# TensorE's order and the order of the weight loads in the emptier experts of a mixture of experts

## The reference

```python
logits = (t @ router)
top_logits, top_idx = lax.top_k(logits, 2)
gates = softmax(top_logits)
for e in range(8):
    out += combine[:, e:e+1] * (silu(t @ w_gate[e]) * (t @ w_up[e])) @ w_down[e]
```

## Time and profile before

| what | value |
|---|---|
| median of three runs | 3641.31 us (3640.61 to 3642.34) |
| the profiled execution's own time | 3644.42 us |
| its span | 3642.5 us |
| mixture of experts, first product to end of the span | 2402 to 3642.5 us |
| TensorE busy, share of the span | 3203.3 us, 88% |
| weights moved by SP's queue | 612.49 MB, most of them in the last third |

### The profile page before, as it was taken

The page is one execution under the profiler, slowest core; times in us unless marked ns, Lnnn a source line. Parts: engine busy times, 40 slices in busy tenths (PEclk is TensorE's granted clock), DMA queues, the critical chain, the costliest instruction groups (busy, mean ns, idle before and its releaser), DMA issues.

```text
span 3642.5 us, 40190 instructions
## 1 busy us (share of the span) xinstructions
PE 3203.3 (88%) x16779; PEld 2258.2 (62%) x16779; DVE 902.0 (25%) x1854; ACT 487.0 (13%) x1111; POOL 106.9 (3%) x115
## 2 busy tenths in 40 slices
PE   7999987999999997996888998989679859958965
PEld 3565666577777774775755777678348537726832
DVE  1677777300101332003651002210000000000000
ACT  1322231100100231002111002210000000000000
POOL 0121121000000000000000000000000000000000
PEclk8999998999999998998989999989889979979987
DMA  6444411344445222442103452179789779889975
GB/s 208 145 161 174 161 54 47 116 148 150 149 151 167 81 70 93 150 138 94 44 12 117 160 184 70 47 266 316 269 287 320 257 256 347 271 270 314 304 244 174
DMA packets 474993, 636.26 MB, mean 175 GB/s; under 512 B 11094, under 2 KB 419261, under 8 KB 467525
## 3 DMA queue, kind: packets, MB, share of 16 engines
q1 hardware_dynamic: 469645, 612.49, 50.4%
q0 software_dynamic: 5184, 21.46, 1.8%
HBM read 632.70 MB, written 1.20 MB: 174 GB/s over the span
## 4 chain that ended last, share of the span: by engine, by line
PE 78%; DMA 7%; DVE 6%; issue 2%; DVEq 2%; ACT 2%; PEld 1%; PEldq 1%; SPq 1%; ACTq 0%; POOL 0%
PE PS L718 28%; PE PS L726 14%; PE PS L3377 7%; PE PS L1071 4%; DMA scratch<-in_moe_wu 3%; PE PS L3409 3%; DMA WO<-in_moe_wu 2%; PE PS L2941 2%; PE PS L541 2%; PE PS L1625 1%; PE PS L1621 1%; DMA WO<-in_ada_w 1%; PE PS L1879 1%; PE PS L1200 1%; PE PS L280 1%
## 5 line engine op out<-in xcount | busy, mean ns | idle before, releaser
L745 DVE TENSOR_TENSOR scratch<-scratch,PS 128x128 f32<-128x128 f32 (+1 forms) x200 | 69.3, 346 | 1410.3 <-ACT scratch L735 1409.9
L718 PE MATMUL PS<-XT,WF 128*128 128x256 f32 x1472 | 324.6, 381 | 1.4 <-ACT XT L486 1.4
L718 PEld LDWEIGHTS PS<-XT,WF 128*128 128x128 f32 x1472 | 281.0, 191 | 51.4 <-issue 12.0
L718 PE MATMUL PS<-XT,WO 128*128 128x256 f32 x1344 | 296.0, 379 | 0.0
L718 PEld LDWEIGHTS PS<-XT,WO 128*128 128x128 f32 x1344 | 255.3, 190 | 49.3 <-issue 16.3
L735 ACT ACTIVATE scratch<-PS 128x128 f32<-128x128 f32 (+1 forms) x200 | 64.8, 324 | 1391.7 <-PE PS L718 1391.7
L3377 PE MATMUL PS<-XT,scratch 128*64 128x256 f32 x512 | 137.5, 431 | 127.8 <-DMA scratch<-in_moe_wu 127.8
L1071 PE MATMUL PS<-XT,WH 128*128 128x512 f32 x512 | 241.5, 599 | 0.0
L726 PE MATMUL PS<-WF,scratch 128*128 128x512 f32 x496 | 224.3, 592 | 0.0
L726 PE MATMUL PS<-WO,scratch 128*128 128x512 f32 x464 | 206.0, 592 | 0.0
L3377 PEld LDWEIGHTS PS<-XT,scratch 128*64 128x64 f32 x512 | 77.6, 157 | 182.4 <-issue 157.1
(11 more groups left out here) (561 smaller groups left out, 4480.2 us busy)
## 6 DMA issues: line engine op xcount, KB each, us to landing
OT<-in_moe_wd SPq DMA_DIRECT2D x56, 1024.0 KB, 9.3
WO<-in_ada_w SPq DMA_DIRECT2D x48, 1024.0 KB, 6.5
WF<-in_moe_wg SPq DMA_DIRECT2D x28, 1024.0 KB, 10.9
WF<-in_moe_wu SPq DMA_DIRECT2D x28, 1024.0 KB, 13.5
WF<-in_moe_wd SPq DMA_DIRECT2D x28, 1024.0 KB, 5.1
WO<-in_moe_wg SPq DMA_DIRECT2D x28, 1024.0 KB, 7.4
WO<-in_moe_wu SPq DMA_DIRECT2D x28, 1024.0 KB, 10.1
WO<-in_moe_wd SPq DMA_DIRECT2D x28, 1024.0 KB, 11.8
```

Of the source, the lines that this page charges most:

```text
L718: mm = nc.tensor.matmul(k.PS[:, 4 + f, w * n:(w + 1) * n], slot.gu[:, w, kb, f * P:(f + 1) * P], rhs(kb), start=kb == 0, stop=kb == KB - 1)
L745: k.nc.vector.tensor_tensor(hid[:, f, :], sg[:, f, :], k.PS[:, 4 + f, n:2 * n], ALU.mult).then_inc(*slots[s].dve.done(f"h{f}"))
```

## The change

In `few_tensor` a turn's gate and up products now stand together, and the same turn's flip and down products follow them before anything of the next turn. The scatter of the expert before stands between up products and flip in the first two turns, the gather of the next expert in the last one. In `moe_sync` the two slots' `gu` loads of a few expert's turn are issued together, and the two `dn` loads after them; the many experts' loads keep their order. No product, transfer or instruction on the other engines is added or removed.

```diff
@@ moe_sync
             for s in range(2):
                 cols = slice((2 * turn + s) * ROUND, (2 * turn + s + 1) * ROUND)
-                gu = [w[:, ds(e, 1), :, cols].rearrange("p e kb n -> p (e kb) n") for w in ups]
-                dn = downs[:, ds(e, 1), 4 * turn + 2 * s:4 * turn + 2 * s + 2, :].rearrange("p e b n -> p (e b) n")
-                load_round(k, sp, slots[s], rnds[s], *gu, dn)
+                gu.append([w[:, ds(e, 1), :, cols].rearrange("p e kb n -> p (e kb) n") for w in ups])
+                dn.append(downs[:, ds(e, 1), 4 * turn + 2 * s:4 * turn + 2 * s + 2, :].rearrange("p e b n -> p (e b) n"))
+            if rank < MANY_RANKS:
+                for s in range(2):
+                    load_ups(k, sp, slots[s], rnds[s], *gu[s])
+                    load_downs(k, sp, slots[s], rnds[s], dn[s])
+            else:
+                for s in range(2):
+                    load_ups(k, sp, slots[s], rnds[s], *gu[s])
+                for s in range(2):
+                    load_downs(k, sp, slots[s], rnds[s], dn[s])
@@ few_up_tensor: both w in one call, the wait always ahead of them
-    if ws[0] == 0:
-        for s in range(2):
-            pe.wait_ge(slots[s].gu_in, (rnds[s] + 1) * 32)
-    for w in ws:
+    for s in range(2):
+        pe.wait_ge(slots[s].gu_in, (rnds[s] + 1) * 32)
+    for w in range(2):
@@ few_tensor
-    few_up_tensor(k, pe, i, 0, range(2))
-    scatter_tensor(k, pe, i - 1, 0)
     for turn in range(E_TURNS):
-        if turn + 1 < E_TURNS:
-            few_up_tensor(k, pe, i, turn + 1, (0,))
+        few_up_tensor(k, pe, i, turn)
+        if turn < 2:
+            scatter_tensor(k, pe, i - 1, turn)
+        last = turn == E_TURNS - 1 and i + 1 < EXPERTS
+        if last:
+            gather_tensor(k, pe, i + 1)
         few_flip_tensor(k, pe, i, turn)
-        if turn + 1 < E_TURNS:
-            few_up_tensor(k, pe, i, turn + 1, (1,))
-        elif i + 1 < EXPERTS:
+        if last:
             gates_turn_tensor(k, pe, i + 1)
         few_down_tensor(k, pe, i, turn)
-        if turn == 0:
-            scatter_tensor(k, pe, i - 1, 1)
-        if turn == E_TURNS - 2 and i + 1 < EXPERTS:
-            gather_tensor(k, pe, i + 1)
```

More of the change, by code:

```diff
@@ L660, in declare_ffn, with load_ups @@
     k.sgm, k.hidm = view(k, 5120, 2, P), view(k, 5376, 2, P)
-def load_round(k, sp, slot, rnd, wg, wu, wd):
+def load_ups(k, sp, slot, rnd, wg, wu):
     sp.wait_ge(*slot.pe.at("up1", rnd - 1))
@@ L667, in load_round, with load_downs @@
         sp.dma_start(slot.gu[:, n, :, :], w).then_inc(slot.gu_in, 16)
+def load_downs(k, sp, slot, rnd, wd):
     sp.wait_ge(*slot.pe.at("down1", rnd - 1))
     sp.dma_start(slot.dn, wd).then_inc(slot.dn_in, 16)
+def load_round(k, sp, slot, rnd, wg, wu, wd):
+    load_ups(k, sp, slot, rnd, wg, wu)
+    load_downs(k, sp, slot, rnd, wd)
 def dense_slots(k, m):
@@ L3285, in moe_sync @@
             slots, rnds = expert_turn(k, i, turn)
+            gu, dn = [], []
             for s in range(2):
                 cols = slice((2 * turn + s) * ROUND, (2 * turn + s + 1) * ROUND)
-                gu = [w[:, ds(e, 1), :, cols].rearrange("p e kb n -> p (e kb) n") for w in ups]
-                dn = downs[:, ds(e, 1), 4 * turn + 2 * s:4 * turn + 2 * s + 2, :].rearrange("p e b n -> p (e b) n")
-                load_round(k, sp, slots[s], rnds[s], *gu, dn)
+                gu.append([w[:, ds(e, 1), :, cols].rearrange("p e kb n -> p (e kb) n") for w in ups])
[9 more added lines that the diff above has]
+                    load_downs(k, sp, slots[s], rnds[s], dn[s])
 def more_sync(k, sp):
@@ L3364, in few_bank, with few_up_tensor @@
     return 4 + (i * E_TURNS + turn) % 2
-def few_up_tensor(k, pe, i, turn, ws):
+def few_up_tensor(k, pe, i, turn):
     slots, rnds = expert_turn(k, i, turn)
     bank = few_bank(i, turn)
-    if ws[0] == 0:
-        for s in range(2):
-            pe.wait_ge(slots[s].gu_in, (rnds[s] + 1) * 32)
-    for w in ws:
+    for s in range(2):
+        pe.wait_ge(slots[s].gu_in, (rnds[s] + 1) * 32)
+    for w in range(2):
         for kb in range(KB):
```

## The result

The changed kernel took 3482.69 us in the median of 4 runs (3481.73 to 3484.48); the kernel before took 3641.82 in 4 runs beside them (3640.61 to 3644.67). The ratio is 0.9563, with a 95% interval of 0.9546 to 0.9579: about 159 us faster. The prediction was 3476, with 3463 to 3503 as its range.

The account below looks back on a forecast made before the run. The order in which TensorE and SP wait for each other was taken as the few experts' bound. Savings of 41.3 us twice and 42.5 twice, 167.6, less 3 for the clock, gave 3644.4 - 165 = 3479, median 3476 us; range 3463 to 3503.

Parts of the forecast that it names:

- The ring: Few experts: TensorE and SP wait for each other, 20 TensorE waits totalling 219.2 us, SP 311.7 us, a lap 23.9 us.
- step 2: SP's load order in few experts: queue has 16 us to spare; the same margins hold with only one edit.
- The transfer's price: Few experts' weight loads: each transfer in a full queue takes 2.90 us, so a turn of six takes 17.4 us.
- The first landing: Third turn of a few expert: its first `gu` transfer lands after 5.4 us, as into an empty queue.
- The clock: Slow start of each few expert's last products after a wait: at most 6.2 us in all, half, 3 us, taken off.
- All before 2402 and after the last product stays.: Parts of the kernel outside the experts: time before 2402 us and after the last product was to stay unchanged.
- The weighed rule: Skill page's advice against products after data waits: every few expert's turn would begin slowly, 1.55 us; sum 3479.
- Slower transfers: Rival, few experts: transfers don't keep 2.90 us; at 3.2 us the time is 3508 us; 9 in 100.
- Clock low throughout: Rival, few experts: all products at 1.2 GHz, a turn 24.1 us, ending at about 3718 us; 4 in 100.
- Starving many experts: Rival, many experts: weights come with less lead, some 5 us lost in each of three, 3491 us; 2 in 100.
- Nothing changes: Rival, few experts: the wait only goes elsewhere, as if 263 GB/s were the traffic's limit; 3641 us; 2 in 100.
- The chains: TensorE's two newly exposed stretches per few expert's turn, before flip and before down products: 1.5 and 0.94 us, costed at nothing.

Follow-up runs that it names:

- e3: Changed kernel with each few expert's down load bringing only the left half of its block, TensorE's work unchanged: 3439.75 us.
- e1: TensorE's new order with SP's old order of loads, so only one of the changed kernel's two edits: 3491.14 us.
- e2: SP's new order of loads with TensorE's old, staggered order, so only the other of the changed kernel's two edits: 3501.89 us.
- three profiled yardsticks: The changed kernel itself, unchanged, run again beside the batches of follow-up runs: 3485.76, 3482.44 and 3483.24 us.
- e4: Changed kernel with products of zeros filling TensorE's breaks in the few experts, ahead of the weight wait and the flip: 3481.91 us.
- e7: Changed kernel with separate gate and up semaphores and both gate blocks loaded ahead of both up blocks, only from a few expert's third turn on: 3465.57 us.
- e6: Changed kernel with separate gate and up semaphores and both gate blocks loaded ahead of both up blocks in every few expert's turn: 3477.61 us.
- e8: e7 with products of zeros added around the gate products of the last turns and ahead of the flip: 3466.57 us.

## Why the prediction was right, and by what it was off

**The ring** was the bound, and breaking it brought what a full queue allows. The 20 waits of 11.0 us are gone; in their place stand 14, nine of 2.0 to 3.9 us and five of at most 1.2, where about 4 an expert of 2 to 4 us were expected; SP's 311.7 us fell to 2.1, the rate rose to 367 GB/s at a share of 1.08, as said. e3 shows that the transfers bind now; e1 and e2 show that either edit suffices to break the ring, as the margins of step 2 said.

**The transfer's price.** 2.86 us instead of 2.90, a turn 17.2 instead of 17.4. The lower bound from the window at 367 GB/s was the better reading than the count of issues. It is a mean over the mixture of a turn, four `gu` of 3.00 us and two `dn` of 2.58.

**The first landing.** From the issue at 2559.05 to the last landing at 2643.28 are 84.2 us where 5.4 + 27 x 2.90 = 83.7 were summed. The first transfer landed at 2565.69, after 6.6 us and not 5.4: it did not enter an empty queue, since two `dn` transfers issued before it landed at 2559.96 and 2562.55. The 27 behind it took 77.6 us and not 78.3. Two mistakes of opposite sign left 0.5 us an expert; that they nearly cancelled is luck.

**The clock** was the mis-sized term. I took off 3 us, half of "at most 1.55 x 4 = 6.2 us", because the waits would be shorter. Shorter waits did not help: in each of the four few experts the last gate and up products took 8.81 us against the 7.2 of the sum, 1.6 each, 6.4 together, slightly over that bound. In the three profiled yardsticks 11 of 12 did the same (8.73 to 8.81), so it was no accident of one execution. e4 takes this away and gets 5.5 us of it back in the few experts. The sum with what was measured: 167.6 - 6.4 (clock) - 2.0 (landing) = 159.2, against 598.0 - 438.5 = 159.5 in the traces and 159.1 between the medians. Of the 6.7 us by which 3476 was too low, the clock is 3.4 and the landing 2.0; the rest is rounding in the forecast and the difference between the medians of the kernel before. Experts of 108 us became 110.3.

**"All before 2402 and after the last product stays."** In the profiled executions the first product of the experts came at 2399.07 instead of 2402.21. The change has no part there; executions of one kernel differ by more than that, as the openings listed above show.

**The weighed rule.** The Trainium skill's page TensorE: Matmul & The Clock Gate, section HAM oscillation, speaks of slow starts after waits for data. The changed kernel's trace agrees for waits of 2.0 to 3.9 us (9 slow turns of 9), and that is where I had discounted it; the 5 turns after waits of at most 1.2 us ran at full clock, so it was not every turn. e1 has turns at full clock after waits of 3.41 and 3.77 us, so no wait's length alone foretells it here, and what else decides stays open. With a slow start of every last turn the sum was to come to 3479; 3482.69 was measured.

**The rivals.** Slower transfers: refuted, 2.86 us. Clock low throughout: refuted, 0.92 to 0.95 over a few expert. Starving many experts: they take 156.2 us (156.2 before), and no wait for a DMA appears on line 727. Nothing changes: refuted. The queue's margins held as well: though SP waited up to 7.4 us ahead of `gu` loads, DMA's share was 1.07 to 1.08 over each of the first three few experts.

**The chains** of 1.5 and 0.94 us showed as waits of 1.6 and 0.6, and cost nothing inside the expert: they lie under the transfers of the next turn. There are 17 waits for VectorE and not 28, because in the other 11 turns a scatter or the gather stands in that place. No run moved scatters and gather alone.

## What to carry to other kernels

When two engines wait for each other in a ring, work out what the resource between them would do with a full queue; that sets the result better than the sum of the waits removed, and breaking the ring at one place brings nearly all of it. Once transfers are the bound, what is left to gain lies behind the last landing of each stretch: put as little work as possible behind it (e7: 3.67 to 5.36 us of products instead of 8.81, 17.7 us in all). When a queue's order is changed, look at the stretch ahead of it as well: a load grouped with another waits for the other's buffer too, and one transfer slipped out of a stretch in which it was free (e6).

## What the runs showed of the hardware

- The clock and the waits can feed each other. In the first few expert a turn with a wait of 3.72 us ahead of it began slowly (8.82 us of gate and up products, granted clock 0.80 over the turn), which used up the next wait (0.48 us), so that the next turn ran at 1.00 (7.13 us) and left a wait of 3.85. In the second, slow starts followed one another at 0.90, with waits of 2.1 us. With breaks of 1.6 and 0.6 us and waits for DMA of at most 1.4 us (e3) it was 1.00 over the whole expert.
- The mean rate of a full queue did not depend on the order of the loads: 366 to 367 GB/s, six transfers of 1 MB in 17.2 us, with four `gu` in a row (the changed kernel), with each slot's `dn` behind its `gu` (e1 and the earlier trace rows) and with the gate blocks first (e6, e7, e8). It did depend on the load: `gu` transfers (runs of 1 KB) landed 3.00 us apart, `dn` transfers (runs of 4 KB) 2.58. The changed kernel's DMA view from 2600 to 2643 us, in 40 slices, shows it as stretches near 350 and near 400 GB/s:

```profile
GB/s 347 350 348 347 349 354 393 397 404 415 392 369 354 350 348 348 349 346 349 351 347 352 387 411 404 408 397 380 345 352 349 350 349 350 346 345 351 362 386 400
```

- With a full queue a transfer takes 11 to 15 us from issue to landing (the last `moe_wu` of the first few expert 11.85), and SP is held 2.8 to 5.9 us at an issue. These times are no cost of issuing: into the nearly empty queue the first transfer of the third turn took 6.6 us and its issue 0.37. The rest are the transfers ahead of it, and they appear as SPq in the chain.
